# A two-stage ConvFFN's opening: another order of job 0, low halves on VectorE alone, norm sums in job 1, and another order at stage and round changes

## The reference

```python
def rmsnorm(x, g):
    y = x * lax.rsqrt(jnp.mean(x * x, axis=-1, keepdims=True) + EPS)
    return y * g
def conv_ffn(xn, buf, w_g, w_u, w_c, b_c, w_d):       # D_MODEL 1024, D_FF 3072, CONV_F 3
    g = xn @ w_g
    gc, new_buf = causal_dwconv(g, buf, w_c, b_c)
    return (jax.nn.gelu(gc) * (xn @ w_u)) @ w_d, new_buf
# per layer: x = x + mixer(rmsnorm(x)); x = x + conv_ffn(rmsnorm(x))
```

## Time and profile before

| | us |
|---|---|
| median of 3 runs (lowest to highest) | 2579.86 (2578.29 to 2581.73) |
| the profiled execution, and its span | 2576.1, 2574.4 |
| TensorE busy (matmuls) | 2466.7, 96% |
| VectorE busy | 1765.6, 69% |
| ScalarE busy | 1148.4, 45% |
| POOL busy | 961.9, 37% |
| mean granted TensorE clock | 0.991 of full |

### The profile page before, as it was taken

The page is one execution under the profiler, slowest core; times in us unless marked ns, Lnnn a source line. Parts: engine busy times, 40 slices in busy tenths (PEclk is TensorE's granted clock), DMA queues, the critical chain, the costliest instruction groups (busy, mean ns, idle before and its releaser), DMA issues.

```text
span 2574.4 us, 46180 instructions
## 1 busy us (share of the span) xinstructions
PE 2466.7 (96%) x18693; PEld 2364.2 (92%) x18693; DVE 1765.6 (69%) x2158; ACT 1148.4 (45%) x1851; POOL 961.9 (37%) x623
## 2 busy tenths in 40 slices
PE   8999998899899999998999999998999999989998
PEld 7888886689899999998999999998999999989998
DVE  7466557645877777777778444637878777787775
ACT  5565756533544444442334433424444444443331
POOL 3234333214445454542223411343545454532221
PEclk9999999999999999999999999998999999999999
DMA  5101106752222232336443211222232222265422
GB/s 183 52 27 51 44 26 217 262 190 77 88 98 103 89 111 80 111 113 243 140 141 93 56 40 37 58 68 90 92 110 86 106 93 98 90 232 199 139 89 82
DMA packets 214178, 276.99 MB, mean 108 GB/s; under 512 B 11438, under 2 KB 158999, under 8 KB 210895
## 3 DMA queue, kind: packets, MB, share of 16 engines
q1 hardware_dynamic: 212910, 271.83, 31.7%
q10 hardware_dynamic: 576, 2.10, 0.2%
q0 software_dynamic: 480, 0.11, 0.0%
HBM read 203.57 MB, written 70.43 MB: 106 GB/s over the span
## 4 chain that ended last, share of the span: by engine, by line
PE 64%; DVE 9%; issue 3%; ACT 1%; POOL 1%; DMA 1%; SPq 0%; DVEq 0%; ACTq 0%; POOLq 0%
PE psum_all L2153 52%; PE psum_all L2810 7%; PE psum_all L148 3%; DVE down_x_ffn L2106 2%; DVE psum_all L2091 1%; DVE x_residual L2519 1%; DVE x_residual L2470 1%; DMA w_raw<-in_w_gate_dram 1%; PE psum_all L2862 0%; PE psum_all L2826 0%; POOL rms_scale L1661 0%; DVE blocks_down L2095 0%; POOL w_lo_part L113 0%; DVE ffn_x_sums L2407 0%; PE psum_all L2850 0%
## 5 line engine op out<-in xcount | busy, mean ns | idle before, releaser
L2153 PE MATMUL psum_all<-ffn_x,blocks 128*128 128x272 f32 x5760 | 737.6, 289 | 22.6 <-DVE ffn_x L2416 13.8
L2153 PEld LDWEIGHTS psum_all<-ffn_x,blocks 128*128 128x128 f32 x5760 | 731.0, 190 | 24.3 <-issue 15.7
L2153 PE MATMUL psum_all<-down_x_ffn,blocks_down 128*128 128x272 f32 x2880 | 376.9, 292 | 24.4 <-DVE x_residual L2519 11.5
L2153 PEld LDWEIGHTS psum_all<-down_x_ffn,blocks_down 128*128 128x128 f32 x2880 | 370.3, 191 | 28.7 <-issue 27.9
L2268 ACT COPY x_residual<-psum_all 128x544 f32<-128x544 f32 x192 | 117.9, 614 | 374.7 <-PE psum_all L2153 371.3
L113 POOL TENSOR_TENSOR w_lo_part<-w_raw,w_hi_part 128x1024 fp32r<-128x1024 f32 x52 | 126.8, 2439 | 355.9 <-ACT w_hi_part L97 355.8
L2519 DVE TENSOR_TENSOR x_residual<-x_residual,psum_all 128x544 f32<-128x544 f32 (+1 forms) x224 | 178.4, 797 | 114.2 <-PE psum_all L2153 112.7
L2470 DVE SCALAR_TENSOR_TENSOR x_residual<-x_residual,ffn_params 128x1088 f32<-128x1088 f32 x96 | 215.2, 2242 | 0.0
L2101 POOL TENSOR_TENSOR x_residual<-x_residual,rms_scale 128x1088 f32<-128x1088 f32 x48 | 153.2, 3191 | 151.7 <-ACT x_residual L2297 151.7
L2455 DVE TENSOR_TENSOR x_residual<-x_residual,psum_all 128x544 f32<-128x544 f32 x144 | 130.1, 904 | 93.2 <-PE psum_all L2153 91.3
L2095 DVE TENSOR_TENSOR blocks<-psum_all,blocks 128x512 fp32r<-128x512 f32 x144 | 99.2, 689 | 121.8 <-ACT blocks L2249 121.8
(11 more groups left out here) (361 smaller groups left out, 4630.1 us busy)
## 6 DMA issues: line engine op xcount, KB each, us to landing
staging_ffn<-hidden_spill SPq DMA_DIRECT2D x54, 816.0 KB, 5.2
hidden_spill<-x_residual SPq DMA_DIRECT2D x24, 1088.0 KB, 4.0
w_raw<-in_w_gate_dram SPq DMA_DIRECT2D x24, 1024.0 KB, 5.4
x_residual<-in_w_up_dram SPq DMA_DIRECT2D x24, 1024.0 KB, 5.2
pages<-in_cache_k_dram SPq DMA_DIRECT2D x64, 256.0 KB, 3.7
pages<-in_cache_v_dram SPq DMA_DIRECT2D x64, 256.0 KB, 4.6
x_spill<-x_residual SPq DMA_DIRECT2D x24, 546.0 KB, 5.4
x_residual<-x_spill SPq DMA_DIRECT2D x24, 546.0 KB, 5.8
```

Source lines behind the costliest of these rows:

```text
L2153: mm = pe.matmul(self.core.ps[:, b + h, 0:HB], wt[:, q * P:(q + 1) * P], xt[:, q, HB * h:HB * (h + 1)], start=first and at == 0, stop=at = ...
```

## The change

What it does, part by part:

- **Last two tiles of the projection.** VectorE makes only S1 and S2 of job 0's blocks before it adds tile 6; the rest, with T1's four sums, two of T3, one of T2, the low of block 4 and T1's whole low half, stands between tiles 6 and 7.
- **Job 0's order** is 1, 2, 0, 4, 3, 5, 6. T products may start before their low half is there (`x_low`: the wait stands ahead of the last third of the matmuls). All T lows are made by VectorE, in one instruction each.
- **Norm sums** go from job 0 to job 1, behind products 1 and 3; the last two squares go to another buffer (`late_sq`), so block 4 no longer waits for them; squares and their addition are written as two halves.
- **Pair 0's convolution** has its own order (`first_pair_dve`, `first_conv_act`): the block work of jobs 1 and 2 first, then scaling and taps. `gate_scale(0, *)`, the gelu of tile 1 and the hidden sums of pair 0 go to job 2.
- **Residual tiles out and back** have a semaphore per tile pair (`x_moved`) instead of one for all.
- **Stage change.** Pieces are split in another order (`FIRST_PIECES`), the last pair's gate scaling goes to job 24, piece 4 of the first ConvFFN is read before the reload, and `down_first` has another order.
- **Round changes.** The next round's T1 low stands behind residual addition 5 instead of 4. The state rows are turned behind product 3 of job 25 instead of 2.

```diff
@@ Output.vector
             if m == KT - 2:
-                self.ffn.first_weights_dve(dve)
-            elif m == KT - 1:
-                self.ffn.open_dve(dve)
+                self.ffn.block_sum(dve, 0, "S1")
+                self.ffn.block_sum(dve, 0, "S2")
...
-            self.ffn.tile_dve(dve, m, KT - 1)
+            if m < KT - 2:
+                self.ffn.tile_dve(dve, m)
+            elif m == KT - 2:
+                self.ffn.open_dve(dve)
@@ Ffn.sync
+        if not self.buf.staging_params:
+            self.load_piece(sp, 4)
         sp.wait_ge(self.gc_ready, FT)
         self.reload(sp, 0)
-        self.load_piece(sp, 4)
+        if self.buf.staging_params:
+            self.load_piece(sp, 4)
@@ Ffn.gpsimd
-        pool.wait_ge(self.act_lead, self.T_HI[T1])
...
-        self.add_squares(pool, KT - 1)
         self.block_lo(pool, 0, 5)
-        pool.wait_ge(self.act_lead, self.T_HI[T3])
...
...
+                if n == 0 and i == 1:
+                    self.add_squares(pool, KT - 1)
-                if up and i in (3, 5):
+                if up and n > 1 and (i == 3 or i == 5 and n < JOBS1 - 1):
                     self.gate_scale(pool, t, (i - 3) // 2)
-                if up and i == 6 and n < JOBS1 - 1:
-                    self.hidden_sum(pool, t, T1)
-                if n and n % 2 == 0 and n < JOBS1 and i == 0:
+                elif n == JOBS1 and i == 1:
+                    self.gate_scale(pool, PAIRS - 1, 1)
+                elif n == 2 and i in (0, 1):
+                    self.gate_scale(pool, 0, i)
+                if up and i == 6 and 1 < n < JOBS1 - 1 or n == 2 and i == 1:
+                    self.hidden_sum(pool, (n - 1) // 2, T1)
+                if n and n % 2 == 0 and n < JOBS1 and i == (1 if n == 2 else 0):
@@ Ffn.opening (TensorE), new
+        def made_first(i):
+            pe.wait_ge(*self.lo_ready(0, i))
+            pe.wait_ge(self.act_lead, self.T_HI[i])
+            self.multiply(pe, 0, i, lambda: pe.wait_ge(self.lead_lo, self.T_LO[i]))
         self.multiply(pe, 0, 1)
         pe.wait_ge(self.out.evac, KT)
+        made_first(T1)
+        pe.wait_ge(self.b_lo, 11)
+        pe.wait_ge(*self.lo_ready(0, 0))
+        self.multiply(pe, 0, 0)
+        pe.wait_ge(self.b_lo, 12)
+        pe.wait_ge(*self.lo_ready(0, 4))
+        pe.wait_ge(self.act_out, 1)
+        self.multiply(pe, 0, 4)
         pe.wait_ge(self.dve_out, 1)
+        made_first(T2)
         pe.wait_ge(self.act_out, 2)
+        made_first(NT4)
         pe.wait_ge(self.act_out, 3)
+        made_first(T3)
@@ Ffn.tensor
+                if n == 1 and i == 5:
+                    pe.wait_ge(self.s_root, 3)
...
+                if n == 1 and i == 1:
+                    pe.wait_ge(self.act_out, 5)
+                    self.sums_pe(pe, (0, 1))
+                elif n == 1 and i == 3:
+                    self.sums_pe(pe, (2,))
@@ Ffn.open_dve, new (behind tile 6; opening_dve follows behind tile 7)
+        self.block_lo(dve, 0, 2)
+        self.tile_dve(dve, KT - 2)
+        self.block_sum(dve, 0, "S4")
+        self.block_lo(dve, 0, 3)
+        self.block_sum(dve, 0, "S3")
+        for q in range(4):
+            self.t1_sum(dve, q)
+        self.t3_sum(dve, 0)
+        self.t3_sum(dve, 1)
+        self.t2_sum(dve, 0)
+        self.block_lo(dve, 0, 4)
+        self.sum_lo(dve, T1)
@@ Ffn.opening_dve, new
+        self.nt4_sum(dve, 0)
+        self.tile_lo(dve, KT - 1, 0, B21, 0)
+        self.t3_sum(dve, 2)
+        self.t3_sum(dve, 3)
+        self.tile_lo(dve, KT - 1, 1, B22, 1)
+        for q in (1, 2, 3):
             self.t2_sum(dve, q)
+        for q in (1, 2, 3):
+            self.nt4_sum(dve, q)
         self.add_out(dve, 0, 1)
+        self.sum_lo(dve, T2)
+        self.sum_lo(dve, NT4)
         self.block_lo(dve, 0, 6)
+        self.add_out(dve, 0, 4)
+        self.sum_lo(dve, T3)
         self.block_sum(dve, 1, "S1")
         self.block_sum(dve, 1, "S2")
         self.block_lo(dve, 1, 2)
         self.block_sum(dve, 1, "S4")
+        self.add_out(dve, 0, 6)
         self.block_lo(dve, 1, 3)
         self.block_sum(dve, 1, "S3")
@@ Ffn.first_pair_dve, new
+        self.block_lo(dve, 1, 4)
+        self.add_out(dve, 1, 1)
+        self.block_lo(dve, 1, 6)
+        self.block_sum(dve, 2, "S1")
+        self.block_sum(dve, 2, "S2")
+        self.block_lo(dve, 2, 2)
+        self.block_sum(dve, 2, "S4")
+        self.block_lo(dve, 2, 3)
+        self.block_sum(dve, 2, "S3")
+        self.scale_dve(dve)
+        self.scale_gate(dve, 0, 0)
+        self.scale_gate(dve, 0, 1)
+        self.conv_tap(dve, o, 0, 0, 1)
+        self.add_out(dve, 1, 4)
+        self.conv_tap(dve, o, 0, 0, 0)
+        self.conv_samples(dve, o, 0, 0)
+        self.block_lo(dve, 2, 4)
+        self.conv_tap(dve, o, 0, 1, 1)
+        self.conv_tap(dve, o, 0, 1, 0)
+        self.conv_samples(dve, o, 0, 1)
+        self.add_out(dve, 1, 6)
+        self.block_lo(dve, 2, 6)
@@ Ffn.vector, pair 1
             self.block_sum(dve, u, "S1")
             self.block_sum(dve, u, "S2")
+            if t == 1:
+                self.hidden_tile(dve, 0, 0)
             self.hidden_tile(dve, t - 1, 1)
             self.add_out(dve, g, 1)
@@ Ffn.opening_act (ScalarE), new
+        for i in range(3):
             self.block_hi(act, 0, i)
+        self.tile_hi(act, KT - 2)
+        self.block_hi(act, 0, 3)
...
         self.block_hi(act, 0, 6)
+        self.square(act, KT - 1)
+        self.copy_out(act, 0, 2)
+        self.sum_hi(act, T2)
         self.copy_out(act, 0, 0)
+        self.sum_hi(act, NT4)
+        self.sum_hi(act, T3)
+        self.block_hi(act, 1, 0)
+        self.block_hi(act, 1, 1)
         self.copy_out(act, 0, 3)
+        self.copy_out(act, 0, 5)
+        for i in range(2, 7):
             self.block_hi(act, 1, i)
+    def first_conv_act(self, act, i):
+        if i == 1:
+            self.roots_act(act, (0, 1))
+        elif i == 3:
+            self.roots_act(act, (2,))
+            self.conv_first(act, 0, 0)
+            self.conv_first(act, 0, 1)
+        elif i == 6:
+            self.gelu(act, 0, 0)
@@ stage change
+    FIRST_PIECES = {(-1, 4): (B21, B11), (-1, 5): (T1,), (-1, 6): (T2,), (0, 1): (NT4,), (0, 2): (T3,)}
@@ Ffn.down_first
         self.piece_lo(dve, 0, T1)
+        self.block_lo(dve, n, 6)
         self.add_residual(dve, n, 0)
+        self.piece_lo(dve, 0, T2)
         self.add_residual(dve, n, 1)
-        self.piece_lo(dve, 0, T2)
+        self.next_sums(dve, n + 1)
         self.piece_lo(dve, 0, B22)
...
@@ Ffn.vector, rounds
-                if turn and i == 4:
+                if turn and i == 5:
                     self.piece_lo(dve, r + 1, T1)
```

More of the change, by code:

```diff
@@ L132, in chunk, with halves @@
     return slice(c * CH, min((c + 1) * CH, USED))
+def halves(tile):
+    return tile.rearrange("p (h n) -> p h n", h=2)
 def width(c):
@@ L1677, in roots_act @@
                            scale=1.0 / D, bias=EPS).then_inc(self.s_root, 1)
+        if 2 not in which:
+            return
         act.wait_ge(self.s_root, 3)
@@ L2255, in copy_out @@
         r, h, name = {0: (0, 0, "d"), 2: (1, 1, "bb"), 3: (0, 1, "a"), 5: (1, 0, "d")}[i]
-        act.wait_ge(self.product, max(self.done(n, k) for k in range(i + 1)))
+        act.wait_ge(self.product, self.done(n, i))
         if t:
@@ L2569, in vector @@
             self.add_out(dve, u, 6)
-            self.block_lo(dve, u + 1, 6)
+            if not last:
+                self.block_lo(dve, u + 1, 6)
         self.down_first(dve)
```

269 lines of the change are left out of this document (116 added, 153 removed).

## The result

The changed kernel takes 2597.41 us (median of 5 runs, 2591.11 to 2598.48) against 2579.86 for the kernel before, run beside it: ratio 1.0063, 95% interval 1.0051 to 1.0075. That is slower by 16 to 17.5 us, where 2581 was predicted. The profiled execution took 2597.41 (span 2595.7, mean granted clock 0.986), so 21.3 us more than the profiled one before.

What follows compares the result with a forecast made beforehand. TensorE, busy in 96% of the span, was taken as the bound. Openings with first pairs +3.0 and +0.4, stage -1.0, rounds -1.2 gave +1.2 on 2576.1: 2577.3, plus 3.8 for the median, 2581; range 2564 to 2591.

Steps and rivals of the forecast that it cites:

- Job 0, -15.0 and -17.3: Opening of each ConvFFN: waits and slow clock gone, job 0 takes 22.4 us instead of 37.3 and 39.8.
- Rival (c): Opening: job 1's w_up load and ScalarE split delay the copy T3's product needs; +2.3 us each, 2586; chance 0.07.
- Job 1, +2.7 each: Job 1 takes over the norm sums (1.6 us), plus waits of 0.6 and 0.5: 23.7 us, +2.7 per ConvFFN.
- Job 2, +15.3 and +15.0: Job 2: waits +7.1 before product 1, +4.8 before product 3, clock +4.0; 37.0 us against 21.7 and 22.0.
- rival (a): Job 2: no port collision and a fast clock, 8.2 us of loss instead of 15.9; 2566; chance 0.22.
- (b): Job 2: the low clock stays from product 1 to 5, costing 5 us more per ConvFFN; 2591; chance 0.16.
- Stage and rounds, -1.0 and -1.2: Change of stage (jobs 23 to 25): -0.5 us per ConvFFN; six changes of round: -0.2 us each.
- Rival (d): Bigger gain at the stage change: bounds -4 and -2.7 us together give 2571; chance 0.10.
- Sum: Whole kernel: all terms together +1.2 us, 2577.3 for the profiled execution, 2581 as a median.

Runs made afterwards that it cites:

- the two orders: Changed kernel with POOL's second gate scaling ahead of the low of job 3's block 1 and VectorE's output 1 addition ahead of the second hidden tile: 2578.70 us, 0.9997.
- filling: Changed kernel with 48 and 34 matmuls whose result is overwritten put into job 2's waits before products 1 and 3: 2585.10 us, ratio 1.0035 to the kernel before.

## Why the prediction was wrong, point by point

- **Job 0, -15.0 and -17.3.** The gain is there: 24.5 us in both. It is 2.1 short. Of that T2's product waits 1.29 instead of 1.0, the last part of T3's 0.75, the third product 0.26, and T2's 24 matmuls take 3.61 instead of 3.16 us at a granted clock of 1.00, since T2's low ends in the midst of them (0.3 of this was forecast). The opening was run on VectorE as if POOL's block lows cost it nothing: T3's low alone lost 1.15. Rival (c) is not the reason: the pause of T3's product is ended by VectorE's low, not by ScalarE's copy.
- **Job 1, +2.7 each: the step that failed.** I had product 1 wait 0.6 us, with no collision there; it waited 2.85 and 2.86 and the clock fell, so job 1 took 28.7 and 27.5 instead of 23.7. In POOL's queue the addition of the last squares stands behind two block lows that wait for ScalarE until 659.33, and so it met S1 of job 1 (3.03 instead of 0.70; those 2.33 us are most of the 2.85). Holding it back alone gave job 1 = 24.9 in both. I had priced the same kind of meeting three times in job 2 and not looked for it in job 1. The clock is the other part: 24 matmuls in 5.78 and 4.77 us, up to 2.6 over.
- **Job 2, +15.3 and +15.0.** Measured 37.1 and 36.7 for 37.0: waits of 6.69 (7.1 forecast) and 4.78 (4.8), the collisions 4.0 (4.5), the clock 2.0 and 2.3 (2.0 and 2.0). Three experiments bear out the parts one by one: POOL held back took 4.0 off the first wait, the two orders took the second away, and filling took the clock's share off both. So neither rival (a), no collision, nor (b), the clock low through job 2, came true. (The terms as written add up to 36.9, not 37.0.)
- **Stage and rounds, -1.0 and -1.2.** -1.8 us together (-4.4 to +0.8) for -2.2. As foreseen, the longest wait at the change of stage moved to product 3 of job 25 (4.68). That the sum came out is partly luck. In the two profiles of before and after, the stretch from product 6 of job 23 to that of job 25 went from 47.9 to 48.7 and from 48.2 to 47.1 us, -0.2 in all for -1.0; the three changes of round gave 1.0 us in the first ConvFFN and 1.5 in the second, -2.6 for -1.2. Rival (d), the bigger gain at the change of stage, did not come; its own bounds, put in place of the -2.2 already in the sum, give 2572.5 and not 2571.
- **Sum.** The misses of jobs 0 and 1 are 2 x 2.1 + 5.0 + 3.8 = 13.0 us; 2581 + 13 = 2594, of 2597.4 measured. The rest, 3 us, is of the size by which the clock differs between executions of the same code. In the profile of the changed kernel, nine jobs in a row of the second ConvFFN (3 to 11) also take 21.14 us instead of 21.00 at a granted clock of 1.00, 1.3 us together; 24 matmuls take 3.18 there and not 3.16. Nine of the other thirteen profiles have such jobs, up to twenty in a row, so they are not put down to the change. The range failed since its upper end was built from the clock in job 2 alone; nothing in it let job 1 cost more.

The port rule of the Trainium skill ("SBUF — State Buffer", section "SBUF: two separate sides"), that VectorE with two SBUF inputs and GpSimd exclude each other for a whole instruction (where the GpSimd operation reads SBUF, as all of these do), fits these rows of the trace: S1 beside the squares 3.03, without them 0.69; a sample operation beside the gate scaling 2.43, without it 0.28.

## What to carry to other kernels

When work is brought forward into a stretch where one engine is nearly full, list every operation of the other engine of a shared port that falls into that stretch, with the time at which its own queue lets it start, before pricing any wait; one displaced operation of some 2.5 us on POOL gave most of a 2.9 us wait, and the clock added 2.6 and 1.6 to it. Ask of each removed wait what is next in the same place: here the sums were behind the addition, the gate scaling behind the convolution, and the store of the hidden sums behind both, and removing more of them gained next to nothing over removing one (0.9987 and 0.9996 after 0.9997) until the last was moved (0.9951). Read the lengths of stages inside a profile, and ratios for the total: 4 us of a difference between two profiled executions was the clock in identical code.
